# The router's normed and turned rows in two tiles used in turns; weights of the third pair of experts loaded at another place in the queue

## The reference, cut to what matters

```python
h = h + _rwkv7_time_mix(...)            # layer 0; layer 1: h + _stick_breaking_attention(...)
h = h + _memory_cross_attention(_rms_norm(h, norm_cross[i]), mem_k, mem_v, xa_wq[i], xa_wo[i])
h = h + _hierarchical_moe(_rms_norm(h, norm_ffn[i]), moe_wg[i], moe_bg[i],
                          moe_we[i], moe_be[i], moe_w1[i], moe_w3[i], moe_w2[i])
...
# in _hierarchical_moe: group logits t @ wg, expert logits t @ we; best group, its two best experts; then
hid = silu(t @ w1[expert]) * (t @ w3[expert]);   y = y + gate * (hid @ w2[expert])
```

## Time and profile before

| what | value |
|---|---|
| median of 3 runs | 1691.88 us (1688.39 to 1696.31) |
| the profiled execution | 1693.46 us |
| its span, first to last instruction | 1691.6 us |
| TensorE busy, weight loads of TensorE busy | 90%, 56% of the span |
| VectorE, ScalarE, GpSimd busy | 47%, 25%, 10% |
| moved by DMA | 315.04 MB, mean 186 GB/s |

### The profile page before, as it was taken

One profiled execution on the slowest core, in us unless ns is written; L12 is line 12 of the kernel. 1 busy time (PEld: TensorE's weight loads), 2 busy tenths in 40 slices (PEclk: granted clock), 3 DMA queues, 4 the chain that ended last, 5 costly groups with the idle time before them and its releaser, 6 DMA issues.

```text
span 1691.6 us, 28991 instructions
## 1 busy us (share of the span) xinstructions
PE 1527.1 (90%) x12509; PEld 943.0 (56%) x12509; DVE 802.5 (47%) x1403; ACT 418.7 (25%) x849; POOL 160.8 (10%) x183
## 2 busy tenths in 40 slices
PE   6999988989999999799788899999999997988777
PEld 4786777777645864534233388646468544333332
DVE  6655555653854355444121455546652544431225
ACT  2124255554201231301000120037321322100002
POOL 2000223230000000111110200000000001111101
PEclk9999999999999999799899999999999997989988
DMA  8208200011631412499999912220042116999995
GB/s 275 100 1 297 71 3 5 4 48 35 226 123 64 191 46 73 161 402 422 424 425 423 349 46 100 100 100 2 1 191 108 54 65 225 405 424 426 423 417 199
DMA packets 82338, 315.04 MB, mean 186 GB/s; under 512 B 17968, under 2 KB 19048, under 8 KB 57312
## 3 DMA queue, kind: packets, MB, share of 16 engines
q1 hardware_dynamic: 70112, 284.86, 43.3%
q0 software_dynamic: 10944, 24.10, 3.9%
q10 hardware_dynamic: 1152, 4.19, 0.6%
HBM read 306.86 MB, written 34.34 MB: 202 GB/s over the span
## 4 chain that ended last, share of the span: by engine, by line
PE 84%; issue 6%; DVE 5%; ACT 3%; DMA 1%; PEld 0%; SPq 0%; ACTq 0%; DVEq 0%; POOLq 0%
PE PS L789 20%; PE PS L2713 15%; PE PS L656 13%; PE PS L1441 9%; PE PS L2738 7%; PE PS L1834 2%; PE PS L1770 2%; PE PS L2698 2%; PE PS L2662 2%; PE PS L627 2%; PE PS L1810 1%; PE PS L2090 1%; PE PS L2111 1%; PE PS L552 1%; PE PS L2101 1%
## 5 line engine op out<-in xcount | busy, mean ns | idle before, releaser
L789 PE MATMUL PS<-arena,ring 128*128 128x256 f32 x1344 | 299.3, 383 | 2.9 <-DVE arena L933 2.9
L789 PEld LDWEIGHTS PS<-arena,ring 128*128 128x128 f32 x1344 | 255.6, 192 | 42.3 <-issue 6.4
L2713 PE MATMUL PS<-ring,arena 128*64 128x512 f32 x512 | 134.9, 687 | 54.4 <-issue 51.3
L656 PE MATMUL PS<-ring,arena 128*128 128x512 f32 x400 | 181.5, 600 | 0.7 <-ACT arena L2056 0.7
L2721 DVE TENSOR_TENSOR arena<-PS,arena 128x256 f32<-128x256 f32 x32 | 13.6, 424 | 253.3 <-PE PS L2728 235.0
L2713 PE MATMUL PS<-arena 128*64 128x512 f32 x512 | 116.3, 607 | 13.5 <-issue 10.7
L2713 PEld LDWEIGHTS PS<-ring,arena 128*64 128x64 f32 x512 | 44.2, 158 | 143.2 <-issue 139.5
L656 PEld LDWEIGHTS PS<-ring,arena 128*128 128x128 f32 x400 | 75.1, 193 | 83.3 <-issue 82.3
L2718 ACT ACTIVATE arena<-PS 128x256 f32<-128x256 f32 x32 | 12.3, 383 | 359.9 <-PE PS L2713 359.9
L838 DVE TENSOR_TENSOR arena<-arena,PS 128x512 f32<-128x512 f32 x56 | 36.8, 684 | 112.5 <-PE PS L789 112.4
L2713 PEld LDWEIGHTS PS<-arena 128*64 128x64 f32 x512 | 40.7, 140 | 87.4 <-issue 83.9
(11 more groups left out here) (336 smaller groups left out, 2248.6 us busy)
## 6 DMA issues: line engine op xcount, KB each, us to landing
arena<-in_moe_w SPq DMA_DIRECT2D x96, 1024.0 KB, 16.2
ring<-in_moe_w SPq DMA_DIRECT2D x96, 1024.0 KB, 14.3
ring<-in_sb_wqkv SPq DMA_DIRECT2D x6, 2048.0 KB, 9.4
ring<-in_xa_wq SPq DMA_DIRECT2D x4, 2048.0 KB, 8.6
ring<-in_xa_wo SPq DMA_DIRECT2D x4, 2048.0 KB, 14.2
ring<-in_xa_wkv SPq DMA_DIRECT2D x3, 2048.0 KB, 10.9
h<-in_x SPq DMA_DIRECT2D x8, 512.0 KB, 8.9
ring<-in_rw_wr SPq DMA_DIRECT2D x2, 2048.0 KB, 11.1
```

What stands on the lines that cost most here:

```text
L656: ins = pe.matmul(PS[:, BANK_OF[g], :], rows(k), cols[:, k, :], start=(k == 0 and not grows), stop=(k == 3), skip_group_check=grows)
L789: ins = pe.matmul(PS[:, BANK_OF[g], M * c:M * c + M], rows[:, k, o:o + P], cols[:, k, :], start=(c + k == 0 and not grows), stop=(k == 3), ...
L2713: ins = pe.matmul(bank(2, 2, F)[r, :, :], xgT[p][:, k, r], w[a][:, :, k, :], start=(k == 0), stop=(k == KC - 1))
```

## The change

`tnE` and `xTE` shrink to two tiles each and move together into pieces 12 to 15; tile t uses place t % 2. So a tile may be written only when the tile two before it is done with: ScalarE now waits for logits of tile t-2 before the turn of tile t (t = 2, 3), for the store of tile 0's rows before the square of tile 2, and for the store of tile 1's rows before tile 3's rows are scaled. The semaphore `rows_out` becomes two, one for each place. Two squares write their unused output elsewhere (`wide_`).

Pieces 16 to 19 are thereby free, and expert 5's up weights (`w13x[1]`) are loaded at the head of `moe_route_loads`, behind the query projection of the cross-attention. In the second layer, where memory keys and values are not needed again after the attention, the down weights of pair 2 go into their pieces 28 to 31 (`w2x`), loaded when the attention's last values are done; `down_weights(2)` is left out there.

```diff
@@ late_evac
+                at_t = t % 2 if name[:3] == "ffn" else t
-                d, v = dst[:, k, P * t:P * t + P], PS[:, late_bank(name, n), 0:P]
+                d, v = dst[:, k, P * at_t:P * at_t + P], PS[:, late_bank(name, n), 0:P]
@@ room
-        tnE = at(12, [NT, C])
-        xTE = at(16, [KC, T])
+        tnE = at(12, [2, C])
+        xTE = at(14, [KC, 2 * P])
+        w2x = [at(28 + 2 * a, [2, C]) for a in range(2)]
@@ moe_route_loads(sp, l)
+            sp.wait_ge(S("proj_filled"), FIRST[f"xq{l}"] + 14)
+            load_up(sp, l, 5, w13x[1], S("w13x_in"))
+            if l == 1:
+                sp.wait_ge(S("proj_filled"), FIRST["xv1"] + 8)
+                for a in range(2):
+                    load_down(sp, l, 4 + a, w2x[a], S("w2_in0"))
             sp.wait_ge(S("proj_filled"), FIRST[f"xo{l}"] + 1)
@@ moe_route_act(act, l), rows(t)
+                if t == 3:
+                    act.wait_ge(S("rows_out1"), 16 * (2 * l + 1))
-                act.activation(tnE[:, t, :], h[:, t, :], ACT.Copy, scale=rstd[:, t:t + 1]).then_inc(S("norm_rows"), 1)
+                act.activation(tnE[:, t % 2, :], h[:, t, :], ACT.Copy, scale=rstd[:, t:t + 1]).then_inc(S("norm_rows"), 1)
@@ moe_route_act(act, l), the loop over t
                 ready(act, t)
+                if t >= 2:
+                    act.wait_ge(S("logits"), NT * l + t - 1)
                 if last:
                     late_evac(act, name, t, xTE, 0, 1)
+                if t == 2:
+                    act.wait_ge(S("rows_out0"), 16 * (2 * l + 1))
                 end, total = 512 if last else C, sumsq[:, t:t + 1]
-                act.activation(tnE[:, t, 0:end], h[:, t, 0:end], ACT.Square, accum_out=total).then_inc(S("ffn_norm"), 1)
+                act.activation(wide_ if last else tnE[:, t % 2, :], h[:, t, 0:end], ACT.Square, accum_out=total)\
+                    .then_inc(S("ffn_norm"), 1)
@@ moe_loads(sp, l), behind the first gather
-            for a in range(2):
-                load_up(sp, l, 4 + a, w13x[a], S("w13x_in"))
+            load_up(sp, l, 4, w13x[0], S("w13x_in"))
...
             up_weights(4)
             up_weights(3)
-            down_weights(2)
+            if l == 0:
+                down_weights(2)
             down_weights(3)
@@ moe_pe, down_pair(n)
+                w = w2x if l == 1 and n == 2 else w2e[p]
-                down(pe, p, 2, 0).then_inc(S("down_half"), 1)
+                down(pe, w, 2, 0).then_inc(S("down_half"), 1)
```

More of the change, by code:

```diff
@@ L2257, in route_logits @@
                 tile_there(pe, f"ffn{l}", t, k)
-                ins = pe.matmul(PS[:, 4, HD * t:HD * t + G + NE], xTE[:, k, P * t:P * t + P], wge[:, k, :],
+                ins = pe.matmul(PS[:, 4, HD * t:HD * t + G + NE], xTE[:, k, P * (t % 2):P * (t % 2) + P], wge[:, k, :],
                                 start=(k == 0), stop=(k == KC - 1))
@@ L2305, in rows @@
                 act.wait_ge(S("ffn_rstd"), 5 * l + (1, 2, 4, 5)[t])
-                act.activation(tnE[:, t, :], h[:, t, :], ACT.Copy, scale=rstd[:, t:t + 1]).then_inc(S("norm_rows"), 1)
+                if t == 3:
+                    act.wait_ge(S("rows_out1"), 16 * (2 * l + 1))
+                act.activation(tnE[:, t % 2, :], h[:, t, :], ACT.Copy, scale=rstd[:, t:t + 1]).then_inc(S("norm_rows"), 1)
                 act.wait_ge(S("norm_rows"), ROWS0[name] + t + 1)
-                act.dma_start(scratch["rows"][P * t:P * t + P, :], tnE[:, t, :]).then_inc(S("rows_out"), 16)
+                act.dma_start(scratch["rows"][P * t:P * t + P, :], tnE[:, t % 2, :])\
+                    .then_inc(S(f"rows_out{t % 2}"), 16)
             act.activation(warm[:, :], gn_eps[:, :], ACT.Sqrt).then_inc(S("table_warm"), 1)
@@ L2328, in moe_route_act @@
                     group_evacuated(act, FIRST[f"xo{l}"] + 12)
-                    act.activation(tnE[:, NT - 1, 512:C], h[:, NT - 1, 512:C], ACT.Square, accum_out=half_sq[:, :])\
+                    act.activation(wide_, h[:, NT - 1, 512:C], ACT.Square, accum_out=half_sq[:, :])\
                         .then_inc(S("ffn_norm"), 1)
@@ L2570, in moe_loads @@
                 load_down(sp, l, 2 + a, w2e[1][a], S("w2_in1"))
-            sp.wait_ge(S("rows_out"), 16 * NT * (l + 1))
+            for t in range(2):
+                sp.wait_ge(S(f"rows_out{t}"), 32 * (l + 1))
             sp.wait_ge(S("logits"), NT * (l + 1))
             sp.wait_ge(S("xg_in0"), 16 * (NPE // 2 * l + 1))
-            for a in range(2):
-                load_up(sp, l, 4 + a, w13x[a], S("w13x_in"))
+            load_up(sp, l, 4, w13x[0], S("w13x_in"))
             def up_weights(n):
@@ L2614, in moe_pool @@
             pool.wait_ge(S("xg_cleared"), 2 * l + 2)
-            pool.wait_ge(S("rows_out"), 16 * NT * (l + 1))
+            for t in range(2):
+                pool.wait_ge(S(f"rows_out{t}"), 32 * (l + 1))
             pool.wait_ge(S("table_ready"), l + 1)
@@ L2732, in hidT_out, with down @@
             return act.activation(hidT[:, :, 0:rows], bank(4, 4, P)[:, 0:2, 0:rows], ACT.Copy)
-        def down(pe, p, n, half):
+        def down(pe, w, n, half):
             for k in range(2):
@@ L2738, in down @@
                     ins = pe.matmul(PS[r, 6 + half, :], hidT[:, k, r],
-                                    w2e[p][a][:, k, 512 * half:512 * half + 512], start=(k == 0), stop=(k == 1))
+                                    w[a][:, k, 512 * half:512 * half + 512], start=(k == 0), stop=(k == 1))
             return ins
@@ L2780, in down_pair @@
                 pe.wait_ge(S("ye_a"), NPE * l + n + l + 1)
-                down(pe, p, 2, 0).then_inc(S("down_half"), 1)
+                w = w2x if l == 1 and n == 2 else w2e[p]
+                down(pe, w, 2, 0).then_inc(S("down_half"), 1)
                 pe.wait_ge(S("ye_v"), NPE * l + n + l + 1)
-                down(pe, p, 2, 1).then_inc(S("down_done"), 1)
+                down(pe, w, 2, 1).then_inc(S("down_done"), 1)
             pe.wait_ge(S("table_ready"), l + 1)
@@ L2933, in body @@
                 step(at_step, 58)
-                down(pe, 0, 1, 0)
-                down(pe, 0, 1, 1).then_inc(st, 1)
+                down(pe, w2e[0], 1, 0)
+                down(pe, w2e[0], 1, 1).then_inc(st, 1)
                 step(at_step, 61)
```

## The result

| | before | changed |
|---|---|---|
| median, 20 runs each | 1691.80 us | 1698.32 us |
| ratio | | 1.0035, 95% interval 1.0025 to 1.0044 |
| span of the profiled execution | 1691.6 us | 1696.2 us |

The change costs 0.35%, 5.9 us (4.2 to 7.4).

The account below looks back on a forecast made before the run. Expert stages end with an unbroken transfer queue, where only bytes behind its last dry moment count; the router passes on short waits. +4.4 - 0.3 - 2.0 = +2.1 us, against the median of 1691.88: 1694.0 us, range 1686 to 1700.

Parts of the forecast that it names:

- the likeliest case: Whole kernel: the forecast itself, +2.1 us, own range +0.5 to +4.4; chance 0.53.
- the third rival, the falling clock: Routers: TensorE's longer idle at tile 2 drops its clock, 1.5 us more a layer, +5.1 in all, 1697.0 us; chance 0.20.
- The wait for tile 0's store: Router, ScalarE before tile 2's square: store lands 2.6 us after issue, square starts 2.2 us later in each layer; +4.4 us.
- I put the whole 2.2 us on the path: Router: nothing idle between ScalarE's late square and tile 1's logits absorbs the delay, so 2 x 2.2 = +4.4 us.
- Other new waits, two semaphores, squares into `wide_`: 0: Router: tile 1's store lands 2.1 us before tile 3's rows are scaled; these waits, semaphores and squares cost 0.
- Expert 5's up weights: -0.3: Both layers, ahead of pair 4's loads: 5.0 us of transfer becomes a longer dry spell; only a shorter tail gains, -0.3 us.
- Pair 2's down weights: -2.0, between 1.0 and 3.3: Second layer's experts: pair 5's loads go out 0.98 us sooner into an empty queue; -2.0 us, gain between 1.0 and 3.3.
- the part about pair 3's wait: Second layer: TensorE's 0.98 us wait before pair 3's up products, read as late weights, should go.
- Bytes count: Expert stages: bound by DMA at 420 GB/s, so every byte removed shortens them; -10.6 us, 1681.3 us; chance 0.11.

Follow-up runs that it names:

- the filled wait: Changed kernel plus 14 TensorE products that nothing reads, just before the transposes that wait for tile 2; 1.0020 against the kernel before.
- the version without the wait: Changed kernel, but tile 2's square writes its unused output into place 1, so only scaling tile 2's rows awaits the store; 1.0001, again 0.9999 against the kernel before.
- the two kernels with an expert cut: Kernel before, loading only an eighth of one expert's up weights in each layer: expert 5 (0.9984) or expert 17 (0.9952).
- the up weights alone: The version without the wait, with pair 2's down weights left at their old place in the queue; 0.9997 against the kernel before.

## Why the prediction came out as it did

The time lay in the range, and the direction of the small shift was right, but the likeliest case was the wrong one: +2.1 us foretold, with +0.5 to +4.4 for its own range, and +5.9 (4.2 to 7.4) measured. It was the third rival, the falling clock (0.20 there), which gave 1697.0 us. That the range held is its width of 14 us, taken for the spread of runs and this rival, and not the forecast.

**The wait for tile 0's store.** Its place, its releaser and its length were right: 2.3 us in the first layer, 2.9 in the second, where the store took 3.1 us instead of 2.6. The Trainium skill (DMA: Bandwidth & Descriptors, Anatomy of one DMA) has a fit for DMAs that GpSimd issues, and 3.2 us for 512 KB is an estimate by it. This store is issued by ScalarE, a case that the fit does not claim, and both landings lie below it.

**The failed step: "I put the whole 2.2 us on the path", and nothing for what follows.** The term was +4.4 us and measures 7.9. In the changed kernel's first layer 4.0 us are 2.3 of waiting, 1.3 of logits at half clock (3.26 against 1.94), and 0.3 for the rest; in the second 4.4 are 2.9 and 1.6 (3.28 against 1.71), to within 0.1. In the kernel before, behind a wait of 1.6 us, the clock was still up for most of the logits; behind one of 3.9 us it was not. The Trainium skill (TensorE: Matmul & The Clock Gate, Part 1: The HAM clock gate) has this fall of the clock behind idle time; the windows agree, and in the filled wait's rows work on TensorE takes it back. I had priced it rightly, at 1.5 us a layer, and given it too small a chance: it happened in both layers of all three kernels that have the wait unfilled, where the 16 instructions of tile 1's logits take 3.46 or 3.47 us each time. In the 18 routers without the added wait they take 1.87 to 3.03 us.

**Other new waits, two semaphores, squares into `wide_`: 0.** Right as far as the rows show. Tile 1's store lands at 701.2 and 1411.6 us in the changed kernel, and tile 3's rows are scaled 2.1 us later in both layers, as foretold. The router of the version without the wait has 32.6 and 31.7 us on the mean of its two runs, the seven other kernels without the wait 31.9 and 31.6.

**Expert 5's up weights: -0.3.** Right in its reason. The bytes turned into a dry spell of some 5 us in the first layer and 6 in the second (a DMA share of 0.04 over 726.5 to 731 us and 0.03 over 1436.5 to 1443), and the two kernels with an expert cut show it from the other side. The first layer's stage did not get shorter: 230.9 and 232.6 us in the two profiles of the changed kernel, 230.7 before.

**Pair 2's down weights: -2.0, between 1.0 and 3.3.** The mean over the runs is -2.0. The 4.5 us of the first profile, which look like more, are one execution. In that profile the reasons given are seen: pair 5's first load goes out 33.3 us behind pair 4's instead of 34.4, and lands in 5.2 us instead of 7.0. But the part about pair 3's wait is no effect of the change alone: the wait was there with the up weights alone, and absent in the version with only the wait added and in those with an expert cut, whose pair 5 loads also go out 33.2 to 33.4 us behind pair 4's. Where the loads are those of before it comes and goes between executions.

**The sum by these terms:** +7.9 - 2.0 = +5.9, against +5.9 and +7.5 measured; terms from single executions make so close a match in part luck. By the same terms the version without the wait should gain 2.0 us and shows none (+0.2 and -0.2, each within 2.9 us). That stays open; the gain of 2.0 rests on stage times of single executions alone.

**"Bytes count"** was rightly rejected: it wanted -10.6 us. Yet the freed room was worth more than the change took from it: used for pair 4's down weights, the kernel took 0.29% less than before.

## What to carry to other kernels

Where a transfer queue is full, bytes counted here only behind its last dry moment; look for what released the first load of the full stretch. If it was room, moving earlier bytes only lengthens the dry spell, and the gain comes from putting a later load into it. When a wait is added in front of TensorE, price the work right behind it at the lower clock too, and see whether the write that forces the wait is one whose output nobody reads.

## What the runs showed that was not expected

Useless products made the router shorter: with 14 of them, 3.25 us on TensorE, it took some 2.4 us a layer less (33.6 and 33.1 us, of one execution, against 36.1 and 35.5).

And the routers without the wait come in two kinds, 30.8 to 31.7 and 32.3 to 32.6 us, nine of each, layer by layer. TensorE's clock goes with them. In all nine shorter ones the 16 instructions of tile 1's logits take 1.87 to 2.25 us, in seven of the nine longer ones 2.41 to 3.03. The version without the wait has one of each; its logits take 2.66 us from 680.60 in the first layer and 1.87 us from 1392.44 in the second (windows as above):

```profile
682.00:688.00 6.00, 6.00 (x18) 3.72 (x18) 3.81 (x19) 1.12 (x4) 0.00 (x0) 0.50 0.00 0
1392.00:1394.50 2.50, 2.27 (x18) 2.20 (x19) 0.08 (x1) 1.01 (x4) 0.00 (x0) 1.00 0.17 70
1395.00:1398.00 3.00, 3.00 (x9) 1.56 (x7) 2.58 (x13) 0.73 (x3) 0.00 (x0) 0.50 0.00 0
1398.50:1401.00 2.50, 2.50 (x13) 1.54 (x12) 2.39 (x8) 1.24 (x3) 0.00 (x0) 1.00 0.90 298
```

The clock is down for all of 682 to 688 us in the longer router; in the shorter one it falls later and is back at 1398.5 us. Why it falls earlier and for longer in one execution than in another stays open, and so do the two longer routers with logits of 1.87 us (first layer, both versions with pair 4's down weights early).
